# A diffusion-transformer layer: modulation in four column chunks with latents accumulated k tile by k tile, and two convolution units placed between the query projection's heads

## The reference

```python
mod_lat = silu(c) @ w_ada + b_ada          # 1024 -> 6*1024, also for c_ctx
sh1, sc1, g1, sh2, sc2, g2 = split(mod_lat)
h  = rmsnorm(x, norm1_g) * (1 + sc1) + sh1      # 512 x 1024
hc = rmsnorm(ctx, norm1_g) * (1 + csc1) + csh1  # 256 x 1024
p, pc = h @ w_in, hc @ w_in[:, :KR_END]
# columns of w_in: [kv latent 256 | rope key 32 | q latent 384 |
#                   conv x 512 | conv B 512 | conv C 512 | gates 2 x 1024]
kn, kr, v = mla_kv(...)    # rmsnorm(kv latent) @ w_ukv, rope on the rope key
qn, qr = mla_query(p, ...) # rmsnorm(q latent) @ w_uq, rope on a part of each head
o = softmax(q k^T) v                       # 512 queries, 768 keys, 8 heads
y_conv = (B * (dwconv3(C * x_in) + conv_b)) @ w_conv_out
x = x + g1 * ((sigmoid(ga) * (o @ w_attn_out) + sigmoid(gc) * y_conv) @ w_o)
x = x + g2 * conv_ffn(rmsnorm(x, norm2_g) * (1 + sc2) + sh2)
out = rmsnorm(x, final_g)
```

## Time and profile before

| | us |
|---|---|
| median of 3 runs | 868.04 (866.25 to 870.66) |
| profiled execution | 869.43 |
| its span | 867.6 |
| TensorE busy | 818.9 (94%) |
| VectorE busy | 487.4 (56%) |
| ScalarE busy | 377.9 (44%) |
| GpSimd busy | 367.1 (42%) |
| mean granted TensorE clock | 0.98 |

### The profile page before, as it was taken

The page is one execution under the profiler, slowest core; times in us unless marked ns, Lnnn a source line. Parts: engine busy times, 40 slices in busy tenths (PEclk is TensorE's granted clock), DMA queues, the critical chain, the costliest instruction groups (busy, mean ns, idle before and its releaser), DMA issues.

```text
span 867.6 us, 11410 instructions
## 1 busy us (share of the span) xinstructions
PE 818.9 (94%) x3960; PEld 678.6 (78%) x3960; DVE 487.4 (56%) x604; ACT 377.9 (44%) x577; POOL 367.1 (42%) x187
## 2 busy tenths in 40 slices
PE   5679968999999999999999899999999999999995
PEld 4457856888888888888768798888888888888884
DVE  5855598788887588887114766555555555000014
ACT  7763346566656532332324455444444444111134
POOL 0095354444543555564523235444444444444420
PEclk9979998999999999999999999999999999999998
DMA  8822211111111488876242124333333333232202
GB/s 303 291 73 60 63 49 50 49 27 47 49 49 26 135 256 266 264 234 202 83 165 70 53 70 126 96 95 97 95 97 97 96 97 96 99 98 96 97 24 97
DMA packets 126238, 96.21 MB, mean 111 GB/s; under 512 B 13468, under 2 KB 111033, under 8 KB 126201
## 3 DMA queue, kind: packets, MB, share of 16 engines
q1 hardware_dynamic: 126169, 95.71, 35.9%
q10 hardware_dynamic: 32, 0.01, 0.0%
HBM read 93.60 MB, written 2.10 MB: 110 GB/s over the span
## 4 chain that ended last, share of the span: by engine, by line
PE 83%; DVE 6%; DMA 2%; issue 2%; POOL 2%; ACT 2%; SPq 1%; ACTq 0%; DVEq 0%
PE ps L368 23%; PE ps L369 23%; PE ps L370 23%; PE ps L1397 7%; PE ps L1379 2%; PE ps L1368 2%; POOL ht L511 2%; DVE work L981 1%; DMA raw<-w_in_dram 1%; PE ps L1454 1%; DVE work L985 1%; DMA xt<-x_dram 1%; DMA xt<-ctx_dram 1%; DVE wlo L312 1%; DVE clo L921 1%
## 5 line engine op out<-in xcount | busy, mean ns | idle before, releaser
L312 POOL TENSOR_TENSOR wlo<-raw,whi 128x1024 fp32r<-128x1024 f32 (+2 forms) x130 | 297.6, 2296 | 438.1 <-ACT whi L304 415.8
L368 PE MATMUL ps<-hhi,whi 128*128 128x512 f32 (+1 forms) x552 | 212.8, 386 | 9.3 <-DVE hlo L921 5.7
L369 PE MATMUL ps<-hlo,whi 128*128 128x512 f32 (+1 forms) x552 | 211.5, 383 | 0.0
L370 PE MATMUL ps<-hhi,wlo 128*128 128x512 f32 (+1 forms) x552 | 211.3, 383 | 0.0
L304 ACT ACTIVATE whi<-raw 128x1024 fp32r<-128x1024 f32 (+2 forms) x131 | 127.5, 982 | 111.8 <-PE ps L370 88.6
L368 PEld LDWEIGHTS ps<-hhi,whi 128*128 128x128 f32 x552 | 105.2, 191 | 30.5 <-DVE hlo L1146 4.0
L370 PEld LDWEIGHTS ps<-hhi,wlo 128*128 128x128 f32 x552 | 105.2, 191 | 20.2
L369 PEld LDWEIGHTS ps<-hlo,whi 128*128 128x128 f32 x552 | 105.3, 191 | 19.8 <-issue 0.2
L1170 DVE SCALAR_TENSOR_TENSOR work<-ps,prm,work 128x511 f32<-128x511 f32 x44 | 33.0, 750 | 74.0 <-ACT work L844 73.1
L1072 DVE SCALAR_TENSOR_TENSOR adacc<-ada,cvec,adacc 128x1024 f32<-128x1024 f32 x28 | 65.1, 2365 | 12.3 <-DMA ada<-w_ada_dram 12.3
L368 PE MATMUL ps<-fhi,whi 128*128 (+1 forms) x176 | 69.2, 393 | 0.1
(11 more groups left out here) (235 smaller groups left out, 1468.1 us busy)
## 6 DMA issues: line engine op xcount, KB each, us to landing
raw<-w_up_dram SPq DMA_DIRECT2D x88, 256.0 KB, 3.1
raw<-w_in_dram SPq DMA_DIRECT2D x66, 256.0 KB, 3.4
ada<-w_ada_dram SPq DMA_DIRECT2D x32, 512.0 KB, 5.8
raw<-w_down_dram SPq DMA_DIRECT2D x44, 256.0 KB, 2.7
adaraw<-w_ada_dram SPq DMA_DIRECT2D x32, 256.0 KB, 5.0
raw<-w_o_dram SPq DMA_DIRECT2D x16, 256.0 KB, 3.1
xt<-x_dram SPq DMA_DIRECT2D x4, 512.0 KB, 6.3
raw<-w_attn_out_dram SPq DMA_DIRECT2D x8, 256.0 KB, 2.7
```

The costliest lines, as they stand in the source:

```text
L312: ins = (engine or nc.gpsimd).tensor_tensor(out=l, in0=r, in1=h.bitcast(F32), op=ALU.subtract)
L368: pe.matmul(o, l[0], r[0], start=start, stop=False)
L369: pe.matmul(o, l[0], r[1], start=False, stop=False)
L370: return pe.matmul(o, l[1], r[0], start=False, stop=stop)
```

## The change

*Head.* The modulation is made in four chunks of 256 shift and 256 gain columns. A unit of `w_ada` now holds two row tiles of one chunk (1 KB rows), so four units complete a chunk, in one bank. The sums leave by one ScalarE copy (`rows`), and four matmuls with the constant `sel` turn them into columns and add high and low parts in one step. Each chunk gives shift and gain for two k tiles of h. The four latent token tiles are loaded and transposed ahead of all weights; the two context tiles come in chunks 1 and 2.

*Latents.* For each k tile the 640 query and key latent columns of `w_in` are loaded as rows (1 KB and 1.5 KB), split by ScalarE, their remainder taken by GpSimd, and TensorE adds this tile's 15 matmuls into five banks at once as soon as its h is there. The key latent of the context is summed after all of that, tile by tile, and the rotary key is cut into two units of four k tiles. The first statistic matmul of the keys now follows the rotary key's projection, and the reciprocal of the key root stands after head 0's rotation.

*Query heads.* After each head TensorE does 6 matmuls of the first two convolution units, x and C of column tile 0; the heads take banks 4 + h % 3. The copy of x stands on ScalarE after head 4, product, middle and taps between the values. The attention turns keep 10 units, in pieces of 12, 8 and 6, with new turns for their steps.

The diff, cut to its core:

```diff
-U_Q = U_ADA + 2 * DT
-U_KV = U_Q + QT
-U_KR = U_KV + KVT
-U_UQ = U_KR + 1
-U_V = U_UQ + HEADS // 2
+U_KR = U_ADA + 2 * DT
+U_UQ = (U_KR + 2, U_KR + 3, U_KR + 5, U_KR + 6)
+U_CX0, U_CC0 = U_KR + 4, U_KR + 7
+U_V = U_KR + 8
...
-CONV_PIECES = ((0, 8), (0, 8), (0, 8), (1, 8), (1, 8), (1, 8), (2, 12), (2, 12))
+CONV_TURNS = ((0, 2, 0, 12), (0, 2, 12, 12)) + tuple(
+    (j, n, at, size) for j in range(1, CT) for n, size in ((0, 8), (1, 8), (2, 6)) for at in range(0, 3 * DT, size))
...
+            for t in range(TT):
+                token_load(t)
+            for n in small_loads:
+                rows_to(*n)
+            for c_ in range(MOD_CHUNKS):
+                for n in range(4):
+                    ada_load(c_, n)
+                latent_load(2 * c_)
+                latent_load(2 * c_ + 1)
+                if c_ in (1, 2):
+                    token_load(TT + c_ - 1)
...
+            query_load(0)
+            query_load(1)
+            conv_load(0, 0)
+            query_load(2)
+            query_load(3)
+            conv_load(0, 1)
...
+            def latent_lo(k):
+
+                pool.wait_ge(s("win_hi"), k + 1)
+                for hi, lo, r in latent_parts(k):
+                    ins = nc.gpsimd.tensor_tensor(out=lo, in0=r, in1=hi.bitcast(F32), op=ALU.subtract)
+                ins.then_inc(s("win_lo"), 1)
...
+            def mod_rows1(c_):
+
+                used(act, 4 * c_ + 3)
+                wait(act, s("cols1_ps"), c_)
+                nc.scalar.activation(rows1[:], ps[0:4, 3, :], ACT.Copy).then_inc(s("rows1"), 1)
...
+            mod_rows1(1)
+            ada_hi(8)
+            latent_hi(2)
+            stream_hi(2)
+            ada_hi(9)
+            latent_hi(3)
+            stream_hi(3)
+            token_rms(4)
+            ada_hi(10)
+            ada_hi(11)
+            mod_rows1(2)
...
+            for u in (U_CX0, U_UQ[2]):
+                split_hi(act, u, u % SLOTS)
...
-                if h in (1, 3):
-                    split_hi(act, U_V + h // 2, (U_V + h // 2) % SLOTS)
...
+                if h in (1, 3, 4, 5):
+                    if h == 4:
+                        conv_x_copy(0)
+                    u = {1: U_UQ[3], 3: U_CC0, 4: U_V, 5: U_N}[h]
+                    split_hi(act, u, u % SLOTS)
...
-            dve.wait_ge(s("k_rms"), 1)
-            nc.vector.reciprocal(sqk[0], sqk[1]).then_inc(s("k_rinv"), 1)
-
-            used(dve, U_KR)
+            used(dve, U_KR + 1)
...
+                if h == 0:
+                    dve.wait_ge(s("k_rms"), 1)
+                    nc.vector.reciprocal(sqk[0], sqk[1]).then_inc(s("k_rinv"), 1)
...
+            def latents(k, tiles):
+
+                pe.wait_ge(s("win_lo"), k + 1)
+                pe.wait_ge(s("h_lo"), k + 1)
+                for m in tiles:
...
+                    last = mm3(pe, ps[:, LATENT_BANK[m], :], w, (hhi[:, k, :], hlo[:, k, :]), k == 0, k == DT - 1)
...
+            for c_ in (2, 3):
+                k = 2 * c_ - 2
+                mod_sums(4 * c_)
+                mod_sums(4 * c_ + 1)
+                latents(k, every)
+                mod_sums(4 * c_ + 2)
+                mod_sums(4 * c_ + 3)
+                latents(k + 1, (0, 1))
+                mod_columns(c_)
+                latents(k + 1, (2, 3, 4))
+                pe.wait_ge(s("mods1"), 4 * c_ + 2)
+                token_columns(TT + c_ - 2)
...
                 last.then_inc(s("q_ps") if h % 2 == 0 else w_used, 1)
+                conv_piece(0, h // 4, h % 4 * 6, 6)
...
-                conv_piece(g)
+                conv_piece(*CONV_TURNS[g])
```

618 lines of the change are left out of this document (378 added, 240 removed).

## The result

The changed kernel takes **885.46 us** (median of 4, 884.18 to 886.63) against 868.19 (866.25 to 870.66) for the kernel before, run beside it: the ratio is 1.0203, with an interval of 1.0184 to 1.0221. It is slower by 17.3 us. The forecast was 875.0, 6.8 slower. The profiled execution took 886.63 with a span of 884.6, against 869.43 and 867.6.

A forecast was written before the change was run, and what follows sets the result against it. It took TensorE to bound the attention turns and VectorE the query stretch, with the head busy with transfers. First scores at 102.4 + 54.4 = 156.8 (+17.3), turns -10.5, net +6.8 on 868.0: about 875 us, range 857 to 887.

The forecast's parts named there:

- the four terms: First query matmul at 102.4, query stretch 54.4, attention turns 10.5 shorter, the rest of the program unchanged.
- The head: Modulation and projections: four rounds, each a loop through four engines ending in a row copy; first query matmul at 102.4.
- The third round: Head, from one row copy to the next: a chain of steps through four engines, summing to 14.3.
- The second: Head, second round: 16.0, with TensorE at the lower clock after idling over 4 us.
- the fourth: Head, fourth round: the third round's chain with one copy out of PSUM more, 14.9.
- The query stretch: From first query matmul to first scores: a loss, 54.4 against 39.0, with two TensorE waits before convolution units.
- the second unit: Query stretch: TensorE waits after head 4 for this convolution unit, ready at 28.3, then 15 slow matmuls of 6.1.
- the first unit's low part: Query stretch: first convolution unit split only after the key norm's root, ready at 7.3; TensorE then idled 4.3.
- the rest, where no line of the change stands: Stages after the attention turns: set aside as unchanged, with no term in the sum.
- Part 1: Attention turns: 48 matmuls leave TensorE, 11.0 us; a gain of 10.5 taken, bounds 6 and 11.
- The third rival: Attention turns: VectorE becomes the bound in single turns, only 2 of the 10.5 come back: 883; chance 0.08.
- the rival of the low clock: Head: TensorE doesn't reach the upper clock in the rounds, a round costs 22 instead of 14.6: 887; chance 0.10.

The follow-up runs named there:

- e5: e4 with ScalarE's copy of the first convolution unit's result moved to head 3, and head 5 put ahead of the second unit on TensorE: 867.7 us.
- e3: Changed kernel with sel padded as in e1 and the two convolution units back in the attention turns, at the kernel before's places: 879.2 us.
- e2: Kernel before with one unused tensor of 8 bytes per partition ahead of small, no instruction changed: 872.8 us.
- e7: Changed kernel with sel padded to 256 bytes per partition, no instruction changed: 878.0 us.
- e4: Kernel before, own head, two convolution units between query heads with the changed kernel's turns, first unit's high part before the key norm's root: 870.7 us.
- e14: Kernel before with GpSimd's low parts of the attention turns' convolution units cut to 32 of 1024 columns, the rest left out: 864.5 us.
- e13: e7 with GpSimd's low parts of the attention turns' convolution units cut to 32 of 1024 columns, the rest left out: 871.5 us.
- e1: Changed kernel with sel padded to 128 bytes per partition instead of 8, no instruction changed: 883.9 us.
- e12: Kernel before with 64 unused bytes per partition between the weights and everything behind them: 874.0 us in one execution.
- e8: Kernel before with 128 unused bytes per partition ahead of all tensors, weights and moving operands alike: 865.8 us in one execution.
- e9: e5 with first taps after the last values, one weight split instead of two ahead of the turns, and three low parts on VectorE: 864.3 us.

## Why the prediction was right and wrong

**Right: the direction and two of the four terms, in part by luck.** The head: four row copies forecast to end at 25.5, 41.5, 55.8 and 70.7, measured 25.1, 39.6, 54.0 and 70.5. The third round, the one worked out step by step, took 14.5 for 14.3, so the chain of a round through four engines is real. The second took 14.4 for 16.0, as the clock was low from 27.7 to 34.5 only (the terms written for it even add up to 16.4), and the fourth 16.4 for 14.9: the two errors cancel. The first query matmul came at 102.03 for 102.4, but at 99.4 to 101.1 in the five other runs with the chunked head, so the agreement within 0.4 is luck and the forecast some 1 to 3 too late. The query stretch took 54.24 for 54.4, and its second half by the steps that the text named: head 4's rotation ended 26.7 after the start for 25.7, and the second unit began 28.0 after it for 28.3. e5 showed that this wait cost 4.7. In the first half, too, the numbers fit: the first unit's low part was ready 6.4 after the start for 7.3, and TensorE idled 3.8 for 4.3. But the prediction let TensorE alone decide there (head 1 ready at 13.4, the reciprocal done at 10.0). Measured they are 11.8 and 11.9, and in e3, with no convolution in the stretch, the late reciprocal and the three banks made it 5.5 longer by themselves.

**Wrong: the rest of the program.** The prediction set aside "the rest, where no line of the change stands", and left it out of the sum, at nothing. It cost 5.5, by an allocation of 8 bytes: e2 brings the loss into the kernel before (4.7), e7 takes it out of the changed one (5.8 of its 7.5 lie there). The step that failed is the premise that a stage without a changed line keeps its time. The diff did show the new tensor.

**Wrong in size: Part 1, "I take 10.5 (bounds 6 and 11)".** It was 5.3, and 6.5 where the low clock was short (e4 and e7). The step that failed is "VectorE would stand at 122 of 142.5: still not the bound on average". VectorE was busy 126.3, since an operation that waits for GpSimd counts as busy, and the average is not what counts: GpSimd's splits hold VectorE up by some 2 us each in single turns, and TensorE then waits. The kernel before lost 1.2 to the splits that e14 cuts, the changed one 7.1, of which 1.7 is a low clock that e13 was spared. Another 1.8 lies at the start of the turns, where the splits now begin 0.4 ahead of the first scores instead of 0.3 behind them, 2.5 in single turns later on, and 1.0 is not accounted for. That the smaller convolution pieces leave TensorE too little to bridge the waits in the later turns is likely and not tested by itself. The third rival named this mechanism, and its condition ("VectorE becomes the bound there in single turns"), but set it down to VectorE's own work and gave it a chance of 0.08.

**The range.** With the distance repaired the changed kernel takes 878.0: between the forecast of 875 and the rival's 883, as the turns were. The measured 885.46 lies within the range of 857 to 887, near the rival of the low clock (887) and for none of its reasons: the rounds were as short as forecast.

## What to carry to other kernels

Before counting matmuls moved off TensorE as time won, look in the trace for operations of the next engine that take three times their usual time, and ask whether what remains on TensorE still hides them. When a change adds or resizes any tensor, compare the durations of matmuls in stages it doesn't touch, and in kernels like these keep moving operands and weights a multiple of 256 bytes apart. A wait of 6.8 us for a copy of 0.57 that is queued behind a long chain is repaired by reordering, here the copy and head 5, not by finding other work. And before repairing a wait, look whether another engine ends at the same moment: of two chains that end together, removing one gains nothing.

## What the runs showed of the hardware

- The distance in SBUF between a matmul's moving operand and its weights changes its time. Matmuls of 512 columns at the upper clock start 0.227 us apart at a distance that is a multiple of 256 bytes, and 0.233 apart with 32 or 128 bytes more (e2, e1, changed kernel); 64 bytes lie between (e12: mean 388 to 397 ns instead of 389 to 393). Moving both together by 128 bytes costs nothing (e8). e8 and e12 are one execution each. Why it is so, the traces don't show; loads of weights overlap the matmuls in all these stages. The Trainium skill ("TensorE: Matmul & The Clock Gate", "Step-by-step: what each phase is for") says that loading the next weights doesn't take read bandwidth from the running matmul; an influence of the distance of nearly 3% is not what one would expect from that.
- An operation of VectorE on one column can take 2.00 us, and a scaling of 0.62 can take 2.76: they end with the GpSimd operation that began before or beside them.
- TensorE's clock fell to the lower level behind idle times of 2.10 us (changed kernel, 156.27; matmuls 0.43 apart from 158.0), 2.26 (e9, 119.10; from 119.7) and 2.98 (e5, 120.71; from 122.0), each time not at once. The earlier trace rows has 2.45 without it. The length of one idle time alone doesn't tell it; to take a stretch as slow after 4 us and as fast after 2.45, as the prediction did, is too simple.
